# A two-block transformer on one core: modulation sums over two chunks, position rows from 128 partitions, inserted pieces ahead of transpositions

## What is computed

```python
for l in range(2):                                  # both layers
    mod = silu(c) @ w_ada[l] + b_ada[l]             # 1 x 6144, twelve chunks of 512 columns
    sh1, sc1, gt1, sh2, sc2, gt2 = split(mod, 6)
    h = x * (1 + sc1) + sh1
    y = token_mixer(h)                              # three branches; A is a differential attention
    x = layernorm(ALPHA * x + gt1 * y)
    x = layernorm(ALPHA * x + gt2 * conv_ffn(x * (1 + sc2) + sh2))
# middle: a gated delta rule, a feed-forward, then a windowed attention of 16 query heads
s = q @ k.T * 64 ** -0.5 + rel_bias[head, bucket(i - j)]   # masked to a window of 128, with sinks
```

## Time and profile before

| | us |
|---|---|
| median of three runs (2810.12 to 2815.71) | 2811.87 |
| the profiled execution | 2810.85 |
| its span, first to last instruction | 2809.0 |
| PE busy | 2603.5 (93%) |
| DVE busy | 2164.8 (77%) |
| ACT busy | 1529.8 (54%) |
| POOL busy | 24.1 (1%) |
| mean granted clock of PE | 0.96 |

### The profile page before, as it was taken

One profiled execution on the slowest core, in us unless ns is written; L12 is line 12 of the kernel. 1 busy time (PEld: TensorE's weight loads), 2 busy tenths in 40 slices (PEclk: granted clock), 3 DMA queues, 4 the chain that ended last, 5 costly groups with the idle time before them and its releaser, 6 DMA issues.

```text
span 2809.0 us, 36257 instructions
## 1 busy us (share of the span) xinstructions
PE 2603.5 (93%) x13810; PEld 2209.0 (79%) x13810; DVE 2164.8 (77%) x2724; ACT 1529.8 (54%) x1824; POOL 24.1 (1%) x46
## 2 busy tenths in 40 slices
PE   7899989998998989989989988899999999999996
PEld 6677769876777789878979876788888888888885
DVE  6877777788867777667676466798988899898886
ACT  2344434543344345455533344577777777777673
POOL 0000000000000000000000000000000000000000
PEclk9989989999999999999999998799999999999998
DMA  9833436676644455543035671698998999899894
GB/s 362 296 135 114 178 122 249 227 286 244 215 156 143 136 198 203 167 160 106 31 111 198 186 237 46 239 364 343 373 360 342 365 369 365 339 372 360 343 359 166
DMA packets 104752, 671.65 MB, mean 239 GB/s; under 512 B 11984, under 2 KB 12240, under 8 KB 27136
## 3 DMA queue, kind: packets, MB, share of 16 engines
q1 hardware_dynamic: 97584, 622.08, 59.8%
q0 software_dynamic: 6992, 47.19, 5.0%
HBM read 665.03 MB, written 4.19 MB: 238 GB/s over the span
## 4 chain that ended last, share of the span: by engine, by line
PE 64%; DVE 23%; ACT 6%; issue 4%; DMA 2%; PEld 0%; DVEq 0%; SPq 0%; ACTq 0%; PEldq 0%
PE bank L857 19%; PE bank L859 19%; PE bank L858 19%; DVE W_low L2317 8%; ACT W_high L1773 3%; PE bank L1291 2%; DVE work L2402 1%; DVE arena L2307 1%; PE bank L1644 1%; DVE work L2634 1%; DMA W<-in_w_layer 1%; DMA W<-in_w_middle 1%; DVE acted L2617 1%; DVE work L2632 1%; DVE arena_parts L2623 1%
## 5 line engine op out<-in xcount | busy, mean ns | idle before, releaser
L2317 DVE TENSOR_TENSOR W_low<-W,W_high 128x1024 fp32r<-128x1024 f32 x426 | 496.5, 1207 | 283.7 <-ACT W_high L1773 278.4
L1773 ACT ACTIVATE W_high<-W 128x1024 fp32r<-128x1024 f32 x426 | 421.6, 1039 | 398.5 <-PE bank L859 192.3
L858 PE MATMUL bank<-W_low,arena_parts 128*128 128x512 f32 (+1 forms) x1128 | 445.2, 395 | 0.0
L857 PE MATMUL bank<-W_high,arena_parts 128*128 128x512 f32 (+1 forms) x984 | 397.3, 404 | 29.0 <-DVE W_low L2317 16.1
L859 PE MATMUL bank<-W_high,arena_parts 128*128 128x512 f32 (+1 forms) x984 | 389.2, 396 | 0.0
L859 PE MATMUL bank<-hT_high,W_low 128*128 128x256 f32 (+2 forms) x1208 | 345.6, 286 | 0.0
L857 PE MATMUL bank<-hT_high,W_high 128*128 128x256 f32 (+1 forms) x1088 | 314.8, 289 | 14.8 <-DVE W_low L2317 14.8
L858 PE MATMUL bank<-hT_low,W_high 128*128 128x256 f32 (+1 forms) x1088 | 309.0, 284 | 0.0
L857 PE MATMUL bank<-W_high,hT_high 128*128 128x512 f32 (+1 forms) x640 | 264.0, 413 | 24.8 <-DVE W_low L2317 10.0
L857 PE MATMUL bank<-arena_parts 128*128 128x512 f32 x672 | 269.5, 401 | 5.3 <-DVE x L3660 3.7
L858 PE MATMUL bank<-W_low,hT_high 128*128 128x512 f32 (+1 forms) x672 | 266.8, 397 | 0.0
(11 more groups left out here) (437 smaller groups left out, 4731.6 us busy)
## 6 DMA issues: line engine op xcount, KB each, us to landing
W<-in_w_layer SPq DMA_DIRECT2D x170, 1024.0 KB, 4.9
W<-in_w_expert SPq DMA_DIRECT2D x148, 1024.0 KB, 5.1
arena<-in_w_expert SPq DMA_DIRECT2D x114, 1024.0 KB, 4.8
W<-in_w_middle SPq DMA_DIRECT2D x58, 1024.0 KB, 5.0
arena<-in_w_layer POOLq DMA_DIRECT2D x40, 1024.0 KB, 7.2
consts<-in_w_expert SPq DMA_DIRECT2D x37, 1024.0 KB, 4.8
R<-in_w_expert SPq DMA_DIRECT2D x37, 1024.0 KB, 4.8
R<-in_rows_layer SPq DMA_DIRECT2D x70, 256.0 KB, 5.9
```

The lines of the kernel that those rows point to most:

```text
L857: mm(bank, lhs[0], rhs[0], start=start, stop=False)
L858: mm(bank, lhs[0], rhs[1], start=False, stop=False)
L1773: do(high_slot(at, w)[:, cols], raw(at, w)[:, cols], ACT.Copy).then_inc(main_highs.filled[main_highs.slot(at, w)], 1)
L2317: tt(lows(at, w)[:, cols], raw(at, w)[:, cols], high_slot(at, w)[:, cols].bitcast(F32), ALU.subtract).then_inc(*low_ready.event(at))
```

## The change

In both layers the sums of chunks 4 and 5, 6 and 7, 8 and 9 are formed in pairs on 1024 columns, 24 steps; the weights are packed to suit, each load having two feature blocks of 1024 columns. The accumulators are `work`, a part of the arena, and `work` again. The places of `sums`, of `ada_in` on DVE and of the row and column products on PE move: 4 and 5 after chunk A2, 6 and 7 after B2, 8 and 9 in unit 4; on DVE 4 and 5 are taken in after B0, 6 and 7 after the first C lowerings. SP loads the bias rows of 4 and 5 after A2's. `relrow` is formed on 128 partitions, eight for each head, and each partition writes 16 rows of `spread`. In the windowed attention the inserted piece stands between scores and transposition (but in unit 10), some pieces and `late_query` are one or two units earlier, the scaling of the residual is in unit 11 instead of 5, the residual additions stand ahead of `w_out`, and a raise stands behind the last eviction.

```diff
@@ -94,7 +94,8 @@
 E_LOADS = 3 * (FFE // 256)
-WOVEN = (0, 2, 4, 5, 7, 9, 10, 11, 12, 13, 14)
+WOVEN = (0, 1, 4, 5, 7, 9, 10, 11, 12, 13, 14)
+LATE_QUERY = {0: (0, 0), 1: (0, 1), 5: (1, 0), 7: (1, 1)}
@@ -107,7 +108,7 @@
 
-    rows = [("A", 0), ("adac", 0), ("lam", 0), ("ada", 4), ("A", 1), ("ada", 5), ("A", 2)]
+    rows = [("A", 0), ("adac", 0), ("lam", 0), ("A", 1), ("A", 2), ("ada", 4), ("ada", 5)]
@@ -503,6 +504,7 @@
         zCg = view(14352, NT, 1024)
+        pair_acc = {4: work[:, :], 6: view(10256, 1024), 8: work[:, :]}
@@ -736,7 +738,8 @@
                         row(due.pop(0)[0])
-                    if name[:2] in R_LOADS[at.part] and name[:2] + (1 - name[2],) not in loads[n:]:
+                    first_pair = name[0] == "ada" and name[1] in (4, 5)
+                    if name[:2] in R_LOADS[at.part] and not first_pair and name[:2] + (1 - name[2],) not in loads[n:]:
@@ -755,6 +758,7 @@
                 after = {("out", 0, 1): [("conv", 0)],
+                         ("A", 2, 1): [("ada", 4), ("ada", 5)],
@@ -827,8 +831,8 @@
             pool.wait_ge(*bias_made.nth(at, 1))
-            pool.dma_start(spread, relrow[0:WQ_HEADS, :].unsqueeze(1).to_broadcast([WQ_HEADS, P, 384])
-                           ).then_inc(bias_out, 16)
+            pool.dma_start(spread.rearrange("h (g r) n -> (h g) r n", r=WQ_HEADS),
+                           relrow.unsqueeze(1).to_broadcast([P, WQ_HEADS, 384])).then_inc(bias_out, 16)
@@ -1054,7 +1058,7 @@
                     a_ = c % 2 * 512 + i * P
-                    last = mm(bank[:, i:i + 1], work[:, a_:a_ + P], ones[:, 0:1], start=True, stop=True)
+                    last = mm(bank[:, i:i + 1], pair_acc[c - c % 2][:, a_:a_ + P], ones[:, 0:1], start=True, stop=True)
@@ -1062,7 +1066,7 @@
                 bank = banks[psum.slot(at, ("ada", c))]
-                acc_ = ada_acc[:, c % 2, :] if c > 9 else work[:, c % 2 * 512:c % 2 * 512 + 512]
+                acc_ = ada_acc[:, c % 2, :] if c > 9 else pair_acc[4][:, c % 2 * 512:c % 2 * 512 + 512]
@@ -1133,9 +1137,10 @@
                     run(chunk((kind, c), (kind, c), hTs, KD, 512, 0 if n == 0 else None, l > 0))
-                    if n in (1, 3, 4, 5):
+                    if n in (2, 5):
                         hand_back()
-                        {1: ada_row, 3: ada_row}.get(n, ada_column)({1: 4, 3: 5, 4: 6, 5: 7}[n])
+                        for c in {2: (4, 5), 5: (6, 7)}[n]:
+                            (ada_row if n == 2 else ada_column)(c)
@@ -1169,9 +1174,10 @@
                         next(bg)
-                        if u in (1, 4):
+                        if u == 4:
                             hand_back()
-                            ada_column(9 if u == 4 else 8)
+                            for c in (8, 9):
+                                ada_column(c)
@@ -1478,7 +1484,7 @@
             bank = banks[psum.slot(at, ("rel", 0))]
-            mm(bank[0:WQ_HEADS, 0:384], R[0:BUCKETS, relb, 0:WQ_HEADS], R[0:BUCKETS, hot, 0:384],
+            mm(bank[:, 0:384], R[0:BUCKETS, relb, 0:P], R[0:BUCKETS, hot, 0:384],
@@ -1567,11 +1573,13 @@
             for u in range(16):
                 if u < 15:
                     window_scores(u + 1)
+                if u in WOVEN and u != 10:
+                    next(weave)
                 if u:
                     window_T(u - 1)
                 if u > 1:
                     window_out(u - 2)
-                if u in WOVEN:
+                if u == 10:
                     next(weave)
             u = 16
             window_T(u - 1)
@@ -2183,13 +2191,14 @@
                 window_exps(u)
                 if u:
                     evict_probsT("W", (u - 1) // NT, (u - 1) % NT, u - 1, 2)
-                if u in (5, 10):
-                    late_query(u // 10)
-                if u in (8, 9, 14, 15):
+                if u in (4, 9):
+                    late_query(u // 9)
+                if u in (8, 9, 14):
                     high(1)
                 if u == 10:
                     high_tiles("woT", 1, woTs)
             evict_probsT("W", 7, 1, 15, 2)
+            high(1)
             high_tiles("woT", 2, woTs, 1)
             high(1)
             raise_slot(0, 0)
@@ -2387,25 +2396,27 @@
 
             def first_steps():
 
-                for c in range(4, 10):
-                    acc = work[:, c % 2 * 512:c % 2 * 512 + 512]
-                    if c > 5:
-                        dve.wait_ge(*psum.full(v.at, ("ada", c - 2)))
+                for c in (4, 6, 8):
+                    acc = pair_acc[c]
+                    if c == 8:
+                        dve.wait_ge(*psum.full(v.at, ("ada", 4)))
+                        dve.wait_ge(*psum.full(v.at, ("ada", 5)))
                     for f in range(KD):
-                        w = ("ada", c, f // 4)
-                        if f % 4 == 0:
+                        w = ("ada", c + f // 4, f // 2 % 2)
+                        if f % 2 == 0:
                             dve.wait_ge(*adas.full(v.at, w))
-                        part = ada_slots[:, adas.slot(v.at, w), f % 4 * 512:(f % 4 + 1) * 512]
+                        part = ada_slots[:, adas.slot(v.at, w), f % 2 * 1024:(f % 2 + 1) * 1024]
                         if f == 0:
                             i = ts(acc, part, csil[:, 0:1], None, ALU.mult)
                         else:
                             i = stt(acc, part, csil[:, f:f + 1], acc, ALU.mult, ALU.add)
                         i.then_inc(dve_done, 1)
                         dve.wait_ge(dve_done, v.count())
-                        if f % 4 == 3:
+                        if f % 2 == 1:
                             dve.nop().then_inc(*adas.frees(v.at, w))
                         if f == KD - 1:
-                            dve.nop().then_inc(*ada_ready.event(v.at))
+                            for _ in range(2):
+                                dve.nop().then_inc(*ada_ready.event(v.at))
                         yield
 
             def ada_steps(l):
@@ -2725,12 +2736,13 @@
                     low(1)
-                    sums(3)
+                    sums(2)
...
                     take_chunk(kind, c, lambda t: z[:, t, c * 512:(c + 1) * 512], ready)
-                    if n in (1, 3, 4, 5):
-                        ada_in({1: 4, 3: 5, 4: 6, 5: 7}[n])
-                    sums(3 if n else 5)
+                    if n == 3:
+                        ada_in(4)
+                        ada_in(5)
+                    sums(1 if n else 2)
@@ -2740,7 +2752,9 @@
                 low(1)
-                sums(2)
+                sums(1)
+                ada_in(6)
+                ada_in(7)
@@ -2851,14 +2865,15 @@
                     stt(scores[:, b, 0, 0:K], scores[:, b, 0, 0:K], rsum[:, b, 0:1],
                                       scores[:, b, 1, 0:K], ALU.mult, ALU.add).then_inc(*probs.event(v.at))
                     dve.wait_ge(*probs.last(v.at))
-                    if u in (2, 4):
-                        ada_in(9 if u == 4 else 8)
+                    if u == 4:
+                        ada_in(8)
+                        ada_in(9)
                     if u % 2 == 0:
                         next(bg)
                     if u:
                         a_out(u - 1)
                     if u < 4:
-                        sums(2)
+                        sums(1)
                     low(1)
                     if u in (2, 3, 4):
                         next(forgets)
@@ -3396,7 +3411,7 @@
             bank = banks[psum.slot(v.at, ("rel", 0))]
-            tt(relrow[0:WQ_HEADS, :], bank[0:WQ_HEADS, 0:384], r[0:WQ_HEADS, 0:384], ALU.add
+            tt(relrow, bank[:, 0:384], r[:, 0:384], ALU.add
@@ -3484,20 +3499,20 @@
                 dve.wait_ge(dve_done, v.count())
                 V.reciprocal(rinv[:, b, :], wsum[:, b, :]).then_inc(*probs.event(v.at))
                 dve.wait_ge(*probs.last(v.at))
+                if u in LATE_QUERY:
+                    late_query(*LATE_QUERY[u])
+                if u > 11:
+                    residual(outs("woa")[u - 12:u - 11], None, ALPHA, False)
                 if u > 1:
                     w_out(u - 2)
                 if u == 9:
                     dve.nop().then_inc(*y_ready.event(v.at))
-                if u in (1, 3, 6, 8):
-                    late_query(u // 6, u // 3 if u < 6 else u // 8)
-                if u == 5:
+                if u == 11:
                     scale_x(v.at, "ln2", 1)
                 if u in (9, 10, 15):
                     low(1)
                 if u == 10:
                     low_tiles("woT", 1, woTs)
-                if u > 11:
-                    residual(outs("woa")[u - 12:u - 11], None, ALPHA, False)
             w_out(14)
             w_out(15)
             dve.nop().then_inc(*rows.frees(v.at, ("sink", 0)))
@@ -3821,6 +3836,9 @@
         ada = _columns(i["w_ada"][l])
+        for c in (4, 6, 8):
+            two = i["w_ada"][l][:, c * 512:(c + 2) * 512].reshape(KD, P, 1024)
```

(3 more changed lines are left out.)

## The result

The changed kernel takes 2792.55 us (median of 4 runs, 2791.47 to 2793.82) beside 2810.99 for the kernel before: a ratio of 0.9934, 95% interval 0.9916 to 0.9951. In a second comparison it was 2793.74 beside 2812.94 (0.9933, 0.9920 to 0.9947). It is 18 to 19 us faster. The profiled execution is 2792.49 us with a span of 2790.4.

What follows compares the result with a forecast made beforehand. TensorE was taken as the bound, near full everywhere, so edits count only where it stood still or ran at the lower clock after a stop. -7.0 - 3.8 + 1.1 = -9.7 us from 2811.87 gave 2802 us, range 2796.5 to 2810.

Steps and rivals of the forecast that it cites:

- Part 2: Modulation sums on 1024 columns in both layers: 48 steps become 24, -1.9 us a layer, -3.8 us in all.
- rival A: The clock comes back too behind the stop at 138 and its layer 1 twin: 5.2 us more, 2797; chance 0.12.
- Part 3: Windowed attention, piece ahead of the transposition and query rows earlier: 7.3 us of stops go, 8.4 paid, net +1.1 us.
- Part 1: Down projection: position rows written from 128 partitions, so no late raises or PE stops, -7.0 us.
- The landing: Write of `spread` in the down projection: 3072 KB expected in 21.6 us at the read back's rate, instead of 35.9.
- the stop of 1.7 us at the modulation rows: First attention: PE waits 1.7 us for step 8 of the sums, before the row products of modulation 4 and 5.
- The +0.8 at B1: Chunk B1 waits for banks that `ada_in` frees behind both additions of B0: PE's stop grows by 0.8 us.
- 7.3 to win: Windowed attention: PE's stops for banks, ScalarE's eviction, query tiles and a raise go, 7.3 us.
- 8.4 to pay: Windowed attention: `w_out` and masks wait behind the piece, 1.4 us at each of six places, 8.4 us.
- B: Write of the position rows isn't faster; its 2048 rows or the DRAM side set its pace: 2809; chance 0.14.
- C: Windowed attention's waits move instead of going: none of 7.3 won, 8.4 paid, 2809; chance 0.18.
- D: Windowed attention: pieces ahead of transpositions hold up masks, `woa` pieces at half clock; stage costs 23.2, 2824; chance 0.06.

Runs made afterwards that it cites:

- z1_ada_early: Changed kernel with TensorE's old windowed-attention order, and the additions of modulation 4 and 5 moved ahead of the first lowering of chunk B0's turn: 2772.8 us (0.9854).
- z3_order_early: Changed kernel with the new TensorE order only at the query pieces (units under 10), the old order at the output pieces: 2787.57 us (0.9907).
- x4_late: Kernel before with only the windowed attention's query rows, scaling, residual rows and last raise moved, second piece at unit 1, TensorE's order as before: 2803.47 us (0.9964).
- z4_query_only: Kernel before with only the windowed attention's query rows moved and the second piece one unit earlier: 2804.63 us (0.9963).
- y4_w32: Kernel before with the position rows written from 32 partitions instead of 16, one run: 2806.07 us.
- x2_sums: Kernel before with only the modulation sums on 1024 columns, in both layers: 2804.5 us (0.9966).
- y1_window: Kernel before with both halves of the windowed attention's edit, order and moved rows, and nothing else: 2809.47 us (0.9988).

## Why the prediction was right or wrong

The step that failed is the same in Parts 2 and 3: the lower clock behind TensorE's stops was given no price in the sum. In Part 2 it was set aside as rival A, in Part 3 it was not asked about, and there the order's cost was also counted on waits that the other half of the edit takes away. The runs showed 8.4 us instead of 3.8 for the sums, 2.4 of it a stop that no step had, and 3.5 won instead of 1.1 lost for the windowed attention.

**Part 1, -7.0: right.** 7.4 measured twice, by the changed kernel's trace and by the run of the write alone. The raises, the missing stops and the overlap with the loads came as told. The landing, estimated at 21.6 us at the read back's rate, took 17.7. By the map of the Trainium skill (SBUF — State Buffer, "Door 1: The DMA port swizzle") 16, 32 and 128 partitions reach 4, 8 and 16 ports. The first step agrees with the runs (35.2 to 19.3 us); the second, which by ports would halve the time again, brought only 2.4 to 3.4 us. The turns of the Trainium skill (DMA: Bandwidth & Descriptors, "Queues, rings and completion order"), by which the loads would get half, fit the trace: from 1585.0 to 1601.8 the write and the loads moved 3.15 and 3.10 MB, and loads issued beside it took up to 9.2 us where the median was 5.0. What didn't follow is the price: no raise waited for a load, and the term stayed at 7.4.

**Part 2, -3.8: the term was too small by 4.6.** The steps are right: 1284 ns for a wide step (1285 told), the stop of 1.7 us at the modulation rows (1.69), the one at the transposition gone. The +0.8 at B1 was 1.7 in layer 0 (3.30 to 5.00) and 0.9 in layer 1 (4.08 to 5.00). Three things were mis-sized.
- The clock behind the transposition. I set it aside as rival A, 0.12, "the attention makes PE stop anyway". From 140 to 160 us it is 1.00 in all seven traces with the wide sums and 0.83 to 0.91 in all seven with the narrow ones; from 730 to 750 in layer 1 likewise. So the rival was the case in the clock.
- The layers together. From 46 to 300 us the wide sums gain 1.5 to 4.6 us on the trace of before (median 1.8 of six, z1_ada_early left out), while kernels with the old layers lose 1.1 (median of seven, before among them), so 2.9; from 640 to 890 it is 2.5 against -1.6, so 4.1. These are 7.0 instead of 3.8. With the stops at B1 as measured the prediction's steps give 2.8 (an estimate: 3.8 less 0.9 and 0.1), so some 4.2 us are left for the clock.
- The stop ahead of the last norm, 2.4 us, which my account of the change did not have: 48 instructions fewer in VectorE's program, and no 16 KB load behind its branch.

7.0 and 2.4 are 9.4, against 8.4 by the medians; the difference is within their spread.

**Part 3, +1.1: the sign was wrong, by 4.6 to 6.** Both prices of the sum were near their single runs: 7.3 to win (9.4 and 9.7 measured), 8.4 to pay (9.9). But I added them. The order's cost was priced at VectorE's five waits for scores and the first output piece; with the query rows early these waits are 2.9 us instead of 14.1, the query pieces cost nothing (z3_order_early) and what is left is 6.2 us. And both prices were counted in stops alone. That they came near is luck: of the 7.3 us of stops to win, 3.8 went (x4_late) and 2.2 (z4_query_only), and 7.4 and 6.9 us of lower clock came on top; of the order's loss in the stage, 5.2 us were stops and 5.5 the clock. TensorE's stops sum to 14.2 us before and 14.1 after, so in stops the net is 0.1, one us from my +1.1; the 5.1 is the clock. The stage moved by 4.9 us at equal instructions and by 5.2 in its window, just at the 5 us that the prediction named as its sign of being wrong. I had looked at the clock in Part 2 only, and it was as plain here: a piece of 24 products took 4.75 us in the trace of before, in a window with the clock at 0.61, and takes 3.13 in the changed kernel's. That window of before:

```profile
1687.50:1692.60 5.10, 5.10 (x29) 4.97 (x30) 2.46 (x9) 2.11 (x9) 0.00 (x0) 0.61 0.01 3
```

**Rivals.** A was the case in the clock; its 5.2 us more are near the 4.2 us estimated above, and its 2797 is still 4 us off, since it left out Part 3's clock and the last stop. B and C are out (y4_w32; z4_query_only). D's mechanism, the piece holding up what stands behind it, is real and is the 6.2 to 9.9 us of the order; with the query rows early it works at the output pieces and not at the query pieces. By the sum over terms: 9.7 told; plus 0.4 in Part 1, 4.6 in Part 2 and 4.6 in Part 3 are 19.3.

## What to carry to other kernels

Price a stop of the engine at the end of the chain with the lower clock behind it, in every stage where the profile shows one, and not as a rival: here a stop of 5.0 us cost 7.0, and a stage with unchanged stops gained 5.1. Two edits of one stage need not add; time the pair and each alone, since the losing half (the order, 6.2 us) hides in the sum. After a change that wins, read its new stops as the next edit: the bank wait at B1, which this change made 1.7 and 0.9 us longer, was worth 14.7 us over both layers.

## What the runs showed of the hardware

- The length of the last stops does not settle the clock behind them. With stops of 1.36 and 0.99 us the first piece of 24 products ran at full clock in x2_sums; with 1.38 and 0.64 it ran at 0.61 in the kernel before. The six kernels with its layers unchanged were 0.8 to 6.3 us behind the kernel before at 890 us. One trace can't tell a change of 3 us from that, and medians of four or five runs have intervals of 7 to 9 us; the 3.5 us of y1_window took ten runs, with an interval of 5.
- A stop of 4.1 to 4.4 us on VectorE, with a branch in it, became 1.85 when 48 instructions fewer stood ahead in its program, and 4.09 with 48 others put back. The eight traces with the long stop have a 16 KB packet of the instruction queue right behind the branch, the six with the short one have none there.
- One transfer of 3072 KB out of 16, 32 and 128 partitions: waits of 35.2, 19.3 and 16.9 us. Out of 16 it kept the DMA engines busy (share 0.96 over the write) at only 216 GB/s, and 1 MB loads beside it took 19 to 21 us; out of 128 they moved 349 GB/s at a share of 0.90, and the loads took up to 9.2 us.
